# Two units of weights to a transfer: 1 MB into two neighbouring slots in place of 512 KB for each unit

## The reference, cut to what matters

```
kv = memn @ w_kv                      # 2048 x 1024, twice
proj = h @ attn_w_in                  # 2048 x 3408
g, u = jnp.split(h @ w_in, 2)         # 2048 x 11264, twice
out = (jax.nn.silu(g) * u) @ w_out    # 5632 x 2048, twice
proj = h @ w_in_2                     # 2048 x 8192 and 8 more columns, twice
```

## Time and profile before

| | |
|---|---|
| Median of three runs | 3159.47 us (3157.63 to 3160.0) |
| The profiled execution's own time | 3158.09 us |
| Its span, first to last instruction | 3156.3 us |
| PE busy | 3092.1 us, 98% of the span |
| DVE, ACT, POOL busy | 1695.8, 1479.6, 218.4 us |
| Data moved by DMA | 542.12 MB, a mean of 172 GB/s |
| Weight loads | 1008, a median of 3.6 to 5.6 us from issue to landing by product |
| Mean granted clock of PE | 0.985 |

### The profile page before, as it was taken

One profiled execution on the slowest core, in us unless ns is written; L12 is line 12 of the kernel. 1 busy time (PEld: TensorE's weight loads), 2 busy tenths in 40 slices (PEclk: granted clock), 3 DMA queues, 4 the chain that ended last, 5 costly groups with the idle time before them and its releaser, 6 DMA issues.

```text
span 3156.3 us, 38550 instructions
## 1 busy us (share of the span) xinstructions
PE 3092.1 (98%) x14368; PEld 2547.0 (81%) x14368; DVE 1695.8 (54%) x1781; ACT 1479.6 (47%) x1835; POOL 218.4 (7%) x205
## 2 busy tenths in 40 slices
PE   8989999999999989899999999999999999999999
PEld 7878888888888778788888888888887788888777
DVE  5654444445445865545445454467454455755444
ACT  6454444444445454554444444454554445556343
POOL 1000000000000220000000000006000000700000
PEclk9999999999999999899999999999999999999899
DMA  8536666665566525366666656666444455644345
GB/s 274 172 112 190 189 189 187 192 187 190 190 192 195 154 86 185 111 189 190 187 192 187 189 189 191 190 188 186 147 147 121 130 184 174 181 146 141 113 143 171
DMA packets 278432, 542.12 MB, mean 172 GB/s; under 512 B 16640, under 2 KB 18720, under 8 KB 277664
## 3 DMA queue, kind: packets, MB, share of 16 engines
q1 hardware_dynamic: 276352, 531.30, 55.6%
q0 software_dynamic: 1952, 9.06, 0.8%
HBM read 537.15 MB, written 3.15 MB: 171 GB/s over the span
## 4 chain that ended last, share of the span: by engine, by line
PE 61%; ACT 2%; DVE 1%; issue 0%; ACTq 0%
PE ps L412 23%; PE ps L441 16%; PE ps L850 15%; PE ps L965 2%; PE ps L1029 2%; PE ps L1007 1%; PE ps L969 1%; ACT w_hi L354 1%; PE ps L949 0%; PE ps L690 0%; PE ps L1646 0%; PE ps L631 0%; PE ps L824 0%; ACT qkT L955 0%; ACT S L995 0%
## 5 line engine op out<-in xcount | busy, mean ns | idle before, releaser
L361 DVE TENSOR_TENSOR w_lo<-w_raw,w_hi 128x1024 fp32r<-128x1024 f32 x1008 | 1269.3, 1261 | 1343.3 <-ACT w_hi L354 1340.1
L354 ACT ACTIVATE w_hi<-w_raw 128x1024 fp32r<-128x1024 f32 x1008 | 1066.8, 1059 | 1548.6 <-PE ps L412 668.3
L850 PE MATMUL ps<-w_hi,actT_hi 128*128 128x512 f32 x1408 | 550.0, 391 | 0.0
L850 PE MATMUL ps<-w_hi,actT_lo 128*128 128x512 f32 x1408 | 548.1, 389 | 0.0
L850 PE MATMUL ps<-w_lo,actT_hi 128*128 128x512 f32 x1408 | 547.8, 389 | 0.0
L412 PE MATMUL ps<-w_hi,hidT_hi 128*128 128x512 f32 x928 | 363.2, 391 | 2.3 <-DVE hidT_lo L659 2.3
L412 PE MATMUL ps<-w_hi,hidT_lo 128*128 128x512 f32 x928 | 361.4, 389 | 0.0
L412 PE MATMUL ps<-w_lo,hidT_hi 128*128 128x512 f32 x928 | 361.1, 389 | 0.0
L441 PE MATMUL ps<-w_hi,actT_hi 128*128 128x512 f32 x768 | 315.5, 411 | 4.1 <-ACT pall L457 3.5
L850 PEld LDWEIGHTS ps<-w_hi,actT_lo 128*128 128x128 f32 x1408 | 264.3, 188 | 55.2
L850 PEld LDWEIGHTS ps<-w_lo,actT_hi 128*128 128x128 f32 x1408 | 264.4, 188 | 54.2
(11 more groups left out here) (259 smaller groups left out, 2795.4 us busy)
## 6 DMA issues: line engine op xcount, KB each, us to landing
w_raw<-ffn_w_in SPq DMA_DIRECT2D x352, 512.0 KB, 3.6
w_raw<-w_in SPq DMA_DIRECT2D x256, 512.0 KB, 3.6
w_raw<-ffn_w_out SPq DMA_DIRECT2D x176, 512.0 KB, 3.9
w_raw<-w_out SPq DMA_DIRECT2D x64, 512.0 KB, 3.8
w_raw<-attn_w_in SPq DMA_DIRECT2D x48, 512.0 KB, 3.7
w_raw<-xattn_w_kv SPq DMA_DIRECT2D x32, 512.0 KB, 5.6
w_raw<-attn_w_out SPq DMA_DIRECT2D x32, 512.0 KB, 3.7
w_raw<-xattn_w_q SPq DMA_DIRECT2D x16, 512.0 KB, 3.6
```

Source lines behind the costliest of these rows:

```text
L354: nc.scalar.activation(w_hi[:, v % NS], w_raw[:, v % NS], ACT.Copy).then_inc(w_hi_done, 1)
L361: nc.vector.tensor_tensor(w_lo[:, v % NS], w_raw[:, v % NS], w_hi[:, v % NS].bitcast(F32), ALU.subtract).then_inc(w_lo_done, 1)
L850: mm = nc.tensor.matmul(ps[:, 2 * b + tb], lhs[:, k, tb * P:(tb + 1) * P], rhs[:, s, kk * CB:(kk + 1) * CB], start=(k == 0 and part == 0), ...
```

## The change

One transfer brings two neighbouring units, into slots s and s + 1. SP waits until both slots are free, that is for the `w_lo` of the second one's predecessor (v - NS + 2 in place of v - NS + 1, with v even). There is one `w_loaded` semaphore for two slots, on which ACT waits for either unit. The layout within a slot is now always 512 columns a row block, also for the narrow product, so PE reads its second row block at `kk * CB`.

```
-        w_loaded = [sem(f"w_loaded{s}") for s in range(NS)]
+        w_loaded = [sem(f"w_loaded{s}") for s in range(NS // 2)]
...
-                    for j in range(li.units):
+                    for j in range(0, li.units, 2):
...
-                            sp.wait_ge(w_lo_done, v - NS + 1 + i * li.body)
+                            sp.wait_ge(w_lo_done, v - NS + 2 + i * li.body)
                         k0 = li.kts[b][UK * j] + (4 * b if name == "pool" else 0)
-                        dst = w_raw[:, v % NS, 0:UK * li.width].rearrange("p (k n) -> p k n", k=UK)
-                        sp.dma_start(dst, li.w[:, k0:k0 + UK, bass.ds(c0, li.width)])\
-                            .then_inc(w_loaded[v % NS], 16)
+                        s = v % NS
+                        dst = w_raw[:, s:s + 2].rearrange("p s (k n) -> p (s k) n", k=UK)[:, :, 0:li.width]
+                        sp.dma_start(dst, li.w[:, k0:k0 + 2 * UK, bass.ds(c0, li.width)])\
+                            .then_inc(w_loaded[s // 2], 16)
...
-            act.wait_ge(w_loaded[v % NS], 16 * (v // NS + 1) + i * (16 * body // NS))
+            act.wait_ge(w_loaded[v % NS // 2], 16 * (v // NS + 1) + i * (16 * body // NS))
...
-                            c = kk * li.width
+                            c = kk * CB
```

## The result

The changed kernel took 3164.73 us (median of 14 runs, 3160.59 to 3170.25), the kernel before 3159.34 us beside it (14 runs, 3157.36 to 3160.69): a ratio of 1.0019, 95% interval 1.0011 to 1.0027, which is 3.5 to 8.5 us slower. The forecast was 7.2 us. The profiled execution is the fastest of the 14 (3160.59 us, span 3158.8), so its end says less than its stages; they are read one by one here.

What follows compares the result with a forecast made beforehand. PE, busy 98% of the span, was taken to bound the kernel. Terms of 2.2 + 0.9 + 1.3 + 0.5 + 2.3 = 7.2 us gave a forecast of 3166.7 us, range 3161 to 3173.

Steps and rivals of the forecast that it cites:

- Price of a load: Every 1 MB weight load: lands 5.0 us after issue, bounds 3.6 and 7.2 us.
- Steady state: Products with ACT and DVE on time: later pair loads stay hidden from PE, costing nothing.
- All the products in which ACT and DVE are on time: The stages to which the claim of no steady-state cost was applied.
- Start: Before PE's first matmul: ACT's first copy waits for the whole pair until 10.0 us, costing 2.2 us.
- The first rival: Start and late places: not slower, losses partly absorbed, load 4.2 us or less; sum 3.4 us, 3162.9 us; chance 0.28.
- Further on in the first products: Units 10 and 19: late pairs delay ACT's copies ahead of norms, costing 0.9 us (0.7 and 0.2).
- Narrow product: Units 346 and 347: late pair delays the block's copy PE waits for, costing 1.3 us, bounds 0 and 3.3.
- `aq0`: Pair 354, 355 comes late for DVE, the late engine there: 0.5 us, bounds 0 and 2.7.
- end of `aq1`: Pair 378, 379 delays the block's copy ahead of the attention: 2.3 us, bounds 0.9 and 4.5.
- the clock as a rival: Around the attention: PE's clock may fall earlier or longer, some 2 us either way; no separate chance given.
- A load of 6 us or more as the usual price: All pair loads: much slower, sum up to 16.2 us, 3170 to 3176 us; chance 0.15.
- A busy queue that gains from larger transfers: First 120 us: larger transfers win at most 2.6 us, giving 3156.9 us; chance 0.05.

Runs made afterwards that it cites:

- e8: The changed kernel, with SP waiting for one more unit's `w_lo` before each pair (v - NS + 3); 4021.86 us, ratio 1.2731 to the kernel before.
- e2: The changed kernel with the first 8 units loaded one by one as before; 3161.34 us, ratio 1.0014 to the kernel before.
- e7: The changed kernel with ACT's last-block copy ahead of the weights copy in `akv_end` and `aq1`, DVE's selection-done signal earlier; 3164.12 us, ratio 1.0017.
- e4: The changed kernel with the first 8 units and units 340 to 383 loaded one by one; 3157.66 us, ratio 1.0002 to the kernel before.
- e5: The kernel before with pairs only for units 376 to 379, at the end of `aq1`; 3160.21 us, ratio 1.0003.
- e3: The changed kernel with units 340 to 383 loaded one by one; 3160.4 us, ratio 1.0006 to the kernel before.
- e1: The kernel before with SP waiting for both slots of a pair, then issuing two 512 KB transfers; 3157.16 us, ratio 0.9997.

## Why the prediction was right, and which terms were off

**Price of a load.** 5.0 us, as taken. The Trainium skill's fit for POOL's path in "DMA: Bandwidth & Descriptors", section "Anatomy of one DMA", gives an estimate of 4.4 us. The measurement decides: on SP's queue 512 KB landed 0.4 us and 1 MB 0.6 us later than estimates by that fit. With 4.4 us the narrow product, `aq0` and the end of `aq1` would all have come out too cheap.

**Steady state.** Nothing in the feed-forward products, as forecast: PE 487.00 of 487 us, and e8 shows the argument's own measure from the other side. "All the products in which ACT and DVE are on time" was too wide: in a mixer stage one pair landed after 7.3 us and PE lost 0.8, a term that the sum put at nothing. The forecast had itself worked out that at 7.2 us a turn has no time to spare (10.7 of 10.9 us), but asked it only of all loads together, not of a single late one.

**Start: 2.2 forecast, 1.3 measured.** The step that was off took unit 1's landing (1.75 + 8.2 = 10.0) for that of the pair. The pair is issued whole at 1.25 and landed after 7.9, at 9.1. The first rival said so ("because nothing is issued between its halves") and charged 1.7.

**Further on in the first products: 0.9 forecast.** In the changed kernel's profile it is 0.05, in e2 0.7, in e7 1.5 and in e4 1.5. The bounds (0 to 2.5) hold all four: whether ACT waits for a pair there differs by execution. That loads of the busy first 100 us took up to 8.2 us was read from the first two alone; in the same profile the next two, of units 2 and 3, took up to 10.6.

**Narrow product: 1.3 forecast, 1.0 measured; `aq0`: 0.5 and 0.6; end of `aq1`: 2.3 and 2.5.** The mechanism is that of the forecast, row by row. e5 makes the last alone, e3 takes the three away. The narrow product was charged 0.4 us for the queue, which the load at 1010.19 (landed at 1015.1, after 4.9) did not have.

**Sum: 7.2 forecast, 6.2 in late starts of PE in the profile, 5.4 between the medians, and 6.0 by the ratio.** That these lie so near one another is partly luck: the clock added 1.6 us in the attention and took 5.3 back later in the profiled execution. The forecast named the clock as a rival of some 2 us either way; in single stages of one execution it was up to 3.1.

**Rivals.** A load of 6 us or more as the usual price is out; single ones took up to 7.3 us in the changed kernel behind its first 100 us. A busy queue that gains from larger transfers is out as well: the first stretch lost time. The first rival was half right: the first pair landed before 10.0, but the price was not under 4.6, and `aq0`, the narrow product and the end of `aq1` cost about what the forecast says. A sum under 6.3 was to be its sign, and the measured ones lie under it, so the sum by itself does not decide between the two; the rows do. "Not slower" stays near: the interval begins at 1.0011, and 0.2% is 1.0020.

## What to carry to other kernels

A transfer for two buffers is ready when its last byte is and can start when its second buffer is free: price both, a unit's time of lead and the longer landing, against the lead that each consumer has, not against the mean bandwidth. In this kernel, whose main engine is 98% busy, the loss sits in the few places where another engine is the late one (the start, a narrow product, a stage with side work on the engine that frees the buffers) and where a wait for a load stands in an in-order queue ahead of work that the main engine needs. Look at such an order first: with one copy of a block ahead of one copy of weights in two places PE waited 2.2 us less, and the kernel was some 4 us faster, where halving the number of transfers lost 5 to 6. How much of the 4 us is the order's own is open, since part of the 2.2 was lost again to the next wait and part of the rest came with the clock. And ask of a ring what one late load does to it, not only what the usual one does.

## What the runs showed of the hardware that was not expected

The granted clock of the same stage was 0.75 or 0.87, 0.79 or 0.89, 0.88 or 0.91 of full speed, and a shift of the work by a few us changed which. In the attentions the falls come behind idle time of PE. In the last mixer stage not all of them do: in the kernel before, PE was busy for 7.44 of the 7.50 us ahead of a fall to the lower level at 2967.6 us. At the end of them it ran small matmuls, on 64 and on 8 rows in place of 128 (the trace models the ends of matmuls, so that its busy time is not quite exact):

```profile
2960.00:2967.50 7.50, 7.44 (x27) 4.40 (x28) 3.80 (x2) 2.98 (x4) 2.40 (x1) 1.00 0.52 148
2967.60:2974.40 6.80, 6.80 (x21) 5.25 (x21) 2.95 (x4) 0.00 (x0) 0.00 (x0) 0.50 0.19 70
```

```profile
2966.08 0.69 PE L969 MATMUL ps<-ncum,ident 8*128 8x256 f32 x2
2966.70 0.70 PE L965 MATMUL ps<-qkT 64*128 64x256 f32 x2
```

That the small matmuls are the cause was not tested. In e5 the 2.3 us lost ahead of the attention had been made up for at the end of the profiled execution (span 3156.0 us, before 3156.3).

The changed kernel's times spread over 9.7 us (3160.59 to 3170.25), those of the kernel before beside it over 3.3. That is not a property of the change: in the 33 runs beside e1 to e4 the kernel before spread over 10.8 us (3149.82 to 3160.59).
